# Pairwise comparisons in a router's top-k selection, and a scatter split around the last up products

## Chip, core and metric

One NeuronCore of a Trainium2 chip runs one program: an inference step of a two-layer decoder in fp32. The metric is the device time of one execution in microseconds.

## What is computed

336 tokens (16 meta and 256 prompt tokens, and 8 sequences of 8 sampled tokens) pass an RWKV-7 layer and a differential attention layer. Each of the two is followed by a mixture of experts (MoE) with the same router:

```python
s = sigmoid(xt @ router_w)                     # (336, 16)
sel = s + router_b
grp = top_k(sel.reshape(-1, 4, 4), 2)[0].sum(-1)   # best two of each group of 4
gmask = one_hot(top_k(grp, 1)[1], 4)           # the best group
eidx = top_k(where(emask, sel, -inf), 2)[1]    # its best two experts
wts = s at eidx, divided by their sum
y = sum over e of gates[:, e] * ((silu(xt @ w_gate[e]) * (xt @ w_up[e])) @ w_down[e])
```

With equal values, the lower index wins. The model width is 1024, an expert's 512. An expert's three matrices have 2 MB each, a layer's 16 experts 100 MB.

## The kernel before, in words

Each engine has its own program, written out by hand, and semaphores join them. The tokens lie in three tiles of 128, 128 and 80 rows (`TOK`). The stages are the RWKV layer, an output projection, MoE 0, keys, values and queries, attention, an output projection, MoE 1 and the output. All parts of the change lie in the two MoE stages, `experts` of each engine.

**In front of the experts.** VectorE (DVE) adds the residual to each tile (`residual`, L2179), from which ACT forms the variance (`spread_of`, L1664) and DVE the normalized rows (`normalize`, L2198). TensorE (PE) turns the tiles (`turn`, L1247) and forms the logits and their fold (`logits`, `route`). ACT takes the sigmoid. DVE's selection (L2334 to L2371) works on 128 x 48 scores, 16 experts for each of three tiles: the sum of the best two of each group as the maximum of six pair sums, then the best group and the best two experts by three calls of `first_best` (L2344), which each take a maximum, mark who equals it, weight the marks by a falling index, take the maximum and compare again. A drain stands behind nearly every small instruction. PE forms the ranks of the tokens within their expert (`ustrict`, `ones`), DVE reads them at L2391, and `select` (L2237) makes from them the 0/1 matrix `SelF`, which for four experts of 64 slots each says which token goes into which slot. Between them, DVE computes two of the remainders (`remainder`, L2287): the normalized rows are held as two fp32r parts, `XTM[0]` (hi, copied by ACT) and `XTM[1]` (lo, what is left); POOL computes the lo part of tile 0. The semaphore `xtm_lo` counts tile 2's, then tile 1's.

**Gather.** `gather(q, i)` (L1109) multiplies the parts by `SelF` into PSUM bank `i % 2`: 12 products of 256 columns, in the order hi 0, 1, 2, lo 0, 2, 1, for two of the eight chunks of the width. Four calls make one quad's input. ACT empties the banks of i = 0 and 2, DVE those of i = 1 and 3 (`gathered`, L1689 and L2242), and call i waits until the bank of i - 2 is empty.

**Experts.** Eight pairs, j = 0 to 7, each of two experts. `pair` of PE (L1173): gate products, up products, then either a scatter or the next gather, then transposes of the product of both (`HH`), of the chosen part of `SelF`, and down products. Every matrix has a slot of 16 KB a partition, seven slots in all, loaded in two halves by SP's queue; a slot is loaded again when PE is through with it (`free`, L543). SP issues in a fixed order: gate, up, down of pair after pair. For the last pair, the down matrices are loaded by halves of their columns.

**Scatter.** The outputs of pairs go back to the rows by products with `SG`, in turns (`TURNS`): pairs (0, 1), (2, 3), (4, 5), (6), (7). One turn has six parts, a tile's half each; PE writes part i into bank 6 + i % 2 once DVE's addition of part i - 2 is done (`scatter`, L1157; `adds`, L2249). Turn 3, that of pair 6, is done in pair 7: PE behind the up products, DVE behind the multiplication of gate and up (L2267). Turn 4 follows the last down products.

## Time and profile before

| | |
|---|---|
| median of 3 runs | 1219.72 us (1216.82 to 1220.41) |
| the profiled execution | 1218.88 us |
| its span | 1217.2 us |
| TensorE busy | 1081.1 us, 89% |
| VectorE busy | 541.1 us, 44% |
| ScalarE busy | 358.0 us, 29% |
| GpSimd busy | 70.0 us, 6% |
| read from HBM | 266.18 MB, 224 GB/s over the span |
| mean granted TensorE clock | 0.937 of full |
| chain that ended last | PE 74%, DVE 12%, DMA 6%, ACT 3% |

Busy shares are means over stages with different limits. The two MoE stages lie at about 412 to 682 us and 937 to 1214 us; the page's slices are 30.4 us each. PEclk and the clock column of the windows are the granted clock as a share of 2.4 GHz: 0.5 is 1.2 GHz. An fp32 product shows as two records of PE. Where a helper issues an instruction, the line is the helper's: L742 is PE's `mm`, L1484 and L1487 are ACT's, L526 is SP's weight load.

### The profile page before, as it was taken

The numbers are of one execution on the slowest core, as the hardware profiler recorded it, in microseconds if no ns is written. First come the engines' busy times: TensorE is split into PE (matmuls) and PEld (weight loads), VectorE is DVE, ScalarE is ACT, GpSimd is POOL, SyncE is SP. The second block draws the span as 40 slices with busy tenths as digits, with TensorE's granted clock in tenths as the row PEclk, the third lists the DMA queues.
The fourth block names the chain that finished last, engine by engine and source line by source line (L and its number), as shares of the span: only waits on it lengthen the run. The fifth ranks groups of instructions, "written<-read, shape, count | busy, mean of one in ns | idle before, by whom it ended". The sixth has DMA issues, their size and how long they took to land.

```text
span 1217.2 us, 23537 instructions
## 1 busy us (share of the span) xinstructions
PE 1081.1 (89%) x10193; PEld 760.0 (62%) x10194; DVE 541.1 (44%) x1068; ACT 358.0 (29%) x720; POOL 70.0 (6%) x101
## 2 busy tenths in 40 slices
PE   4989989899888869999998799999879599999984
PEld 3877978899855644555443699976636444444532
DVE  5856536556566571212122754474444631222215
ACT  3435424443232421111111533473232411111102
POOL 2002100011000000000000112011100000000000
PEclk8989979999997979999999899999989699999997
DMA  9503010011041929999999803464733289999991
GB/s 333 215 10 69 19 47 3 3 38 38 25 154 70 396 95 421 422 422 423 422 423 398 316 1 125 159 234 144 290 139 140 106 348 422 423 423 423 422 401 48
DMA packets 58251, 274.16 MB, mean 225 GB/s; under 512 B 5169, under 2 KB 5690, under 8 KB 34082
## 3 DMA queue, kind: packets, MB, share of 16 engines
q1 hardware_dynamic: 48160, 237.58, 48.6%
q0 software_dynamic: 9360, 34.72, 8.8%
q8 instruction: 83, 1.36, 0.5%
q10 hardware_dynamic: 626, 0.32, 0.1%
q14 instruction: 22, 0.18, 0.0%
HBM read 266.18 MB, written 6.46 MB: 224 GB/s over the span
## 4 chain that ended last, share of the span: by engine, by line
PE 74%; DVE 12%; DMA 6%; ACT 3%; issue 2%; DVEq 1%; SPq 0%; POOLq 0%; ACTq 0%; POOL 0%
PE ps L742 69%; DMA arena<-in_moe_w_up 5%; ACT arena L1484 2%; PE ps L883 1%; PE ps L1373 1%; DVE arena L1924 1%; DMA arena<-in_cache_k 1%; ACT arena L1487 1%; PE ps L1089 1%; PE ps L1205 1%; DVE pwr_lo L1930 0%; PE ps L1253 0%; DVE arena L2024 0%; DMA arena<-in_x_prompt 0%; DVE arena L2483 0%
## 5 line engine op out<-in xcount | busy, mean ns | idle before, releaser
L742 PE MATMUL ps<-arena 64*64 64x64 f32 (+10 forms) x7348 | 625.8, 323 | 61.8 <-DVE arena L2376 15.6
L742 PEld LDWEIGHTS ps<-arena 64*64 64x64 f32 (+4 forms) x7348 | 355.5, 140 | 309.1 <-issue 220.7
L1487 ACT COPY arena<-ps 128x512 f32<-128x512 f32 (+7 forms) x294 | 121.4, 432 | 338.8 <-PE ps L742 182.2
L2267 DVE TENSOR_TENSOR arena<-arena,ps 128x512 f32<-128x512 f32 x16 | 17.4, 1085 | 185.5 <-PE ps L742 185.5
L1484 ACT ACTIVATE arena<-ps,arena 128x256 f32<-128x256 f32 (+5 forms) x96 | 45.5, 507 | 133.5 <-PE ps L742 102.4
L2278 DVE SCALAR_TENSOR_TENSOR yy_lo<-ps,arena,yy_hi 128x512 fp32r<-128x512 f32 x32 | 22.7, 747 | 123.0 <-ACT yy_hi L1484 123.0
L1484 ACT ACTIVATE pw_hi<-arena 128x1024 fp32r<-128x1024 f32 x40 | 42.0, 1057 | 89.0 <-PE ps L742 82.8
L742 PE MATMUL ps<-px_hi,pw_hi 128*128 128x336 f32 x192 | 63.4, 330 | 1.4 <-DVE px_lo L2157 1.0
L742 PE MATMUL ps<-px_lo,pw_hi 128*128 128x336 f32 x192 | 61.9, 322 | 0.0
L742 PE MATMUL ps<-px_hi,pw_lo 128*128 128x336 f32 x192 | 61.8, 322 | 0.0
L1484 ACT ACTIVATE yy_hi<-ps,arena 128x512 fp32r<-128x512 f32 x32 | 20.5, 684 | 106.3 <-PE ps L742 106.3
L1484 ACT ACTIVATE arena<-arena 128x1024 f32<-128x1024 f32 (+9 forms) x73 | 42.9, 629 | 26.9 <-DVE arena L2176 20.6
L2146 DVE TENSOR_TENSOR pw_lo<-arena,pw_hi 128x1024 fp32r<-128x1024 f32 x24 | 29.4, 1225 | 43.2 <-ACT pw_hi L1484 43.1
L742 PE MATMUL ps<-rx_hi_hi,pwr_hi 128*128 128x336 f32 x96 | 34.3, 357 | 12.6 <-ACT rx_hi_hi L1484 8.0
L742 PE MATMUL ps<-yy_hi,sg 128*128 128x512 f32 (+1 forms) x96 | 40.4, 421 | 4.8 <-DVE arena L2256 2.7
L1930 DVE TENSOR_TENSOR pwr_lo<-arena,pwr_hi 128x1024 fp32r<-128x1024 f32 x24 | 29.4, 1223 | 33.8 <-ACT pwr_hi L1484 33.6
L742 PE MATMUL ps<-pw_hi,px_hi 128*128 128x512 f32 (+1 forms) x96 | 40.7, 424 | 4.1 <-ACT pw_hi L1484 3.8
L1484 ACT ACTIVATE arena<-ps 128x512 f32<-128x512 f32 (+4 forms) x23 | 11.4, 506 | 103.9 <-PE ps L742 103.8
L742 PE MATMUL ps<-pw_hi,px_lo 128*128 128x512 f32 (+1 forms) x96 | 39.6, 413 | 0.0
L742 PE MATMUL ps<-pw_lo,px_hi 128*128 128x512 f32 (+1 forms) x96 | 39.3, 409 | 0.0
L742 PEld LDWEIGHTS ps<-px_hi,pw_hi 128*128 128x128 f32 x192 | 37.1, 193 | 1.9 <-issue 1.9
L742 PE MATMUL ps<-yy_lo,sg 128*128 128x512 f32 (+1 forms) x96 | 37.8, 394 | 0.0
(229 smaller groups left out, 1387.3 us busy)
## 6 DMA issues: line engine op xcount, KB each, us to landing
arena<-in_moe_w_gate SPq DMA_DIRECT2D x64, 1024.0 KB, 15.7
arena<-in_moe_w_up SPq DMA_DIRECT2D x64, 1024.0 KB, 18.8
arena<-in_moe_w_down SPq DMA_DIRECT2D x64, 1024.0 KB, 17.0
arena<-in_rwkv_w_rkv SPq DMA_DIRECT2D x6, 2048.0 KB, 19.5
arena<-in_w_kv_shared SPq DMA_DIRECT2D x4, 2048.0 KB, 19.8
arena<-in_cache_k POOLq DMA_DIRECT2D x16, 512.0 KB, 4.6
arena<-in_cache_v POOLq DMA_DIRECT2D x16, 512.0 KB, 6.8
arena<-in_rwkv_w_out SPq DMA_DIRECT2D x2, 2048.0 KB, 10.3
```

The lines of the kernel that those rows point to most:

```text
L742: return pe.matmul(out, lhsT, rhs, start=start, stop=stop)
L883: m = pe.transpose(ps[:, b + hf, P * c:P * c + P], src[:, 4 * hf + c, o0:o0 + P], ident)
L1089: m = pe.transpose(ps[0:n, 4 + g % 4, P * c:P * c + P], X[:, 4 * hf + c, t0:t0 + n], ident)
L1205: m = pe.transpose(ps[:, 2, P * f:P * f + P], HH[:, P * f:P * f + P], ident)
L1373: m = pe.transpose(ps[:, 2 * g + hf, P * c:P * c + P], PGK[b % 4][:, g, P * (4 * hf + c):P * (4 * hf + c) + P], ident)
L1484: return act.activation(out, in_, func, **k)
L1487: return act.copy(out, in_)
L1924: stt(X[:, c, :], sgT[:, c, :], mixv[m][:, c:c + 1], xT[:, c, :], ALU.mult, ALU.add).then_inc(S("mix_ready"), 1)
L1930: tt(lo, w_in(L_RKV + n // 4)[:, :, P * (n % 4):P * (n % 4) + P], hi.bitcast(F32), ALU.subtract).then_inc(S("rw_lo"), 1)
L2146: tt(lo, w_in(L_KV + co // 4)[:, :, P * (co % 4):P * (co % 4) + P], hi.bitcast(F32), ALU.subtract).then_inc(S("pw_lo"), 1)
L2267: tt(HH.rearrange("p (k q) -> p q k", k=NF), HS.rearrange("p (q k) -> p q k", k=NF), bank(3).rearrange("p (q k) -> p q k", k=NF), ALU.mult ...
L2278: stt(YY[ROWS[j]][1][:, h], bank(4 + hf), gsl, YY[ROWS[j]][0][:, h].bitcast(F32), ALU.mult, ALU.subtract).then_inc(S("yl_ready"), 1)
```

## The change

Five edits, in both layers:

1. The selection compares every value with the other three of its set: `r4` holds "other > own", `g4` "other >= own", and where the other comes first `g4` replaces `r4` by a predicated copy; the sum over the others is the rank. This is done once for groups (rank below 0.5 is the best group), and once for the experts of the best group, which a product with the mask and a sum over groups picks out (rank below 1.5; -1 for rows beyond the tile). The three calls of `first_best` and the masking with large numbers go.
2. The remainders of tiles 2 and 1 on DVE move behind `select`, ahead of the counts.
3. The first two calls of the first gather are interleaved: four parts of both banks, then lo 2 of both behind the first `xtm_lo`, then lo 1 of both behind the second.
4. Residual 2 moves ahead of the normalization of tile 0 on DVE, and the variance of tile 2 ahead of the first copy of turned rows on ACT.
5. In pair 7, parts 0 to 2 of turn 3 of the scatter go ahead of the up products on PE, and ahead of the multiplication on DVE; parts 3 to 5 stay.

```diff
@@ constants and sizes @@
+PARTS = [(0, 0), (0, 1), (0, 2), (1, 0), (1, 2), (1, 1)]
-    parts["w16"], parts["w4"], parts["valid"]
+    parts["first"] = np.tile((np.arange(4)[None, :] < np.arange(4)[:, None]).reshape(1, 16), (P, 1))
+    parts["below"] = np.concatenate([np.where(p < n, 1.5, -1.0) for _, n in TOK], 1)
@@ PE gather @@
-            def gather(q, i):
-                for h, t in ((0, 0), (0, 1), (0, 2), (1, 0), (1, 2), (1, 1)):
+            def gather(q, i, order):
+                for h, t in order:
                     t0, k = TOK[t]
-                    if q % 4 == 0 and i == 0 and h and t:
-                        pe.wait_ge(S("xtm_lo"), 2 * (q // 4) + (1 if t == 2 else 2))
...
-                m.then_inc(S("xg_mm"), 1)
+                if order[-1] == (1, 1):
+                    m.then_inc(S("xg_mm"), 1)
@@ PE scatter, pair @@
-            def scatter(l, s):
+            def scatter(l, s, first=0, end=6):
...
-                for i, (t, hf) in enumerate(parts(s)):
+                for i, (t, hf) in list(enumerate(parts(s)))[first:end]:
...
                     if k == 1:
                         wait(pe, S("sg_ready"), g)
+                        if j == PAIRS - 1:
+                            scatter(l, 3, 0, 3)
...
                 if j == PAIRS - 1:
-                    scatter(l, 3)
+                    scatter(l, 3, 3, 6)
@@ PE experts @@
-                for i in range(4):
-                    if i >= 2:
-                        pe.wait_ge(S(("xga_ready", "xgb_ready")[i % 2]), 8 * l + i // 2)
-                    gather(4 * l, i)
+                for i in range(2):
+                    gather(4 * l, i, PARTS[0:4])
+                pe.wait_ge(S("xtm_lo"), 2 * l + 1)
+                for i in range(2):
+                    gather(4 * l, i, PARTS[4:5])
+                pe.wait_ge(S("xtm_lo"), 2 * l + 2)
+                for i in range(2):
+                    gather(4 * l, i, PARTS[5:6])
+                for i in range(2, 4):
+                    pe.wait_ge(S(("xga_ready", "xgb_ready")[i % 2]), 8 * l + i // 2)
+                    gather(4 * l, i, PARTS)
@@ ACT experts @@
                 spread_of(2 * l, 1)
+                spread_of(2 * l, 2)
                 turned_copy(l, 0)
-                spread_of(2 * l, 2)
@@ DVE adds, pair: first and end as in scatter @@
+                if j == PAIRS - 1:
+                    adds(l, 3, 0, 3)
                 dve.wait_ge(S("hs_ready"), g + 1)
...
                 if j == PAIRS - 1:
-                    adds(l, 3)
+                    adds(l, 3, 3, 6)
@@ DVE experts @@
                 residual(l, 1)
+                residual(l, 2)
                 normalize(2 * l, 0)
-                residual(l, 2)
...
+                def ahead(val):
+                    other = v3(val).unsqueeze(2).to_broadcast([P, 3, 4, 4])
+                    own = v3(val).unsqueeze(3).to_broadcast([P, 3, 4, 4])
+                    tt(g44(r4), other, own, ALU.is_gt)
+                    tt(g44(g4), other, own, ALU.is_ge)
+                    dve.drain()
+                    dve.copy_predicated(v3(r4), mc("first").bitcast(U32).unsqueeze(1).to_broadcast([P, 3, 16]), v3(g4))
+                    dve.drain()
+                    dve.tensor_reduce(ga, g12(r4), AX, ALU.add)
+                    dve.drain()
...
-                first_best(gb, gm, ga, G_, mc("w4"))
-                gmask = gb.unsqueeze(2).to_broadcast([P, 12, 4])
-                tsc(gc, gb, BIG, -BIG, ALU.mult, ALU.add)
-                tt(g12(a1), g12(sel), gmask, ALU.mult)
-                dve.drain()
-                tt(g12(a1), g12(a1), gc.unsqueeze(2).to_broadcast([P, 12, 4]), ALU.add)
-                dve.drain()
-                first_best(msk0, a1, a2, E_, mc("w16"))
-                stt(a1, msk0, -2 * BIG, a1, ALU.mult, ALU.add)
-                dve.drain()
-                first_best(oh, a1, a2, E_, mc("w16"))
-                tt(msk, msk0, oh, ALU.add)
-                dve.drain()
-                tt(v3(msk), v3(msk), mc("valid").unsqueeze(2).to_broadcast([P, 3, E_]), ALU.mult)
+                ahead(gm)
+                tsc(gb, ga, 0.5, None, ALU.is_lt)
+                dve.drain()
+                tt(g12(a1), g12(sel), gb.unsqueeze(2).to_broadcast([P, 12, 4]), ALU.mult)
+                dve.drain()
+                dve.tensor_reduce(v3(gm), a1.rearrange("p (t g n) -> p t n g", t=3, g=4), AX, ALU.add)
+                dve.drain()
+                ahead(gm)
+                tt(v3(gc), v3(ga), mc("below").unsqueeze(2).to_broadcast([P, 3, 4]), ALU.is_lt)
+                dve.drain()
+                tt(g44(msk), v3(gb).unsqueeze(3).to_broadcast([P, 3, 4, 4]), v3(gc).unsqueeze(2).to_broadcast([P, 3, 4, 4]), ALU.mult)
...
                 tsc(a2, msk, -1e6, 1e6, ALU.mult, ALU.add)
-                remainder(2)
                 dve.wait_ge(S("rt_pe"), 5 * l + 5)
...
                 select(4 * l)
+                remainder(2)
+                remainder(1)
                 dve.tensor_reduce(cntp[:, 0:1], ps[:, 7, 64:80], AX, ALU.max)
...
                 dve.drain().then_inc(S("route_ready"), 1)
-                remainder(1)
```

## Rows read from the trace of the kernel before

**Rows 1.** The page: the span, and what the transfers moved in 40 slices.

```profile
span 1217.2 us, 23537 instructions
...
GB/s 333 215 10 69 19 47 3 3 38 38 25 154 70 396 95 421 422 422 423 422 423 398 316 1 125 159 234 144 290 139 140 106 348 422 423 423 423 422 401 48
```

**Rows 2.** Windows, MoE 0: busy time of the engines, PEclk, DMA share, GB/s.

```profile
430.40:431.20 0.80, 0.00 (x0) 0.00 (x0) 0.58 (x4) 0.00 (x0) 0.00 (x0) 0.50 0.05 20
...
458.00:646.00 188.00, 188.00 (x1007) 93.41 (x1003) 37.42 (x53) 26.16 (x53) 0.54 (x1) 1.00 1.01 423
```

**Rows 3.** The chain that ended last, MoE 0's last pair: start, length, what.

```profile
620.89 29.45 DMA arena<-in_moe_w_up
...
650.38 8.79 PE ps L742 x30
...
659.26 1.08 DVE arena L2267
660.34 0.53 DVE arena L2254
...
661.01 0.72 PE ps L742 x2
...
662.59 1.25 PE ps L742 x4
```

**Rows 4.** Timeline of VectorE in MoE 0: selection, weights, remainder, ranks (start, length).

```profile
427.02 0.17 DVE L2346 TENSOR_REDUCE arena<-arena 128x3 f32<-128x12 f32 x1
...
429.22 0.20 DVE L2346 TENSOR_REDUCE arena<-arena 128x3 f32<-128x48 f32 x1
429.50 0.21 DVE L2348 TENSOR_TENSOR arena<-arena 128x48 f32<-128x48 f32 x1
...
432.88 0.17 DVE L2373 COPY arena<-arena 128x16 f32<-128x16 f32 x1
...
434.35 0.21 DVE L2385 TENSOR_TENSOR arena<-arena 128x48 f32<-128x48 f32 x1
434.48 0.18 DVE L2387 TENSOR_SCALAR arena<-arena 128x48 f32<-128x48 f32 x1
434.57 1.89 DVE L2292 TENSOR_TENSOR xtm_lo<-arena,xtm_hi 80x1024 fp32r<-80x1024 f32 x1
436.56 0.20 DVE L2391 TENSOR_TENSOR arena<-arena,ps 128x48 f32<-128x48 f32 x1
```

**Rows 5.** Timeline of MoE 0: ranks, gather, first evacuation, first gate products.

```profile
433.44 1.46 PE L742 MATMUL ps<-arena 128*128 128x48 f32 x6 [7.79 <-DVE arena L2376]
...
437.94 1.62 PE L742 MATMUL ps<-sel,xtm_hi 128*128 128x256 f32 x6 [3.04 <-DVE sel L2239]
...
441.15 1.02 ACT L1484 ACTIVATE arena<-ps,arena 128x256 f32<-128x256 f32 x2 [11.63 <-PE ps L742]
...
443.12 0.88 PE L742 MATMUL ps<-sel,xtm_hi 128*128 128x256 f32 x6
...
447.30 3.22 PE L742 MATMUL ps<-arena 128*64 128x512 f32 x14 [1.14 <-issue]
```

**Rows 6.** Timeline of MoE 0: normalization and turning of tiles 0 and 1.

```profile
415.71 0.81 DVE L2202 TENSOR_SCALAR arena<-arena 128x1024 f32<-128x1024 f32 x1
...
416.44 0.68 DVE L2187 SCALAR_TENSOR_TENSOR arena<-arena,ps 80x512 f32<-80x512 f32 x1
...
416.58 1.10 PE L1253 MATMUL ps<-arena 128*128 128x128 f32 x8 [1.82 <-DVE arena L2202]
...
419.03 1.97 PE L1253 MATMUL ps<-arena 128*128 128x128 f32 x8 [1.36 <-DVE arena L2202]
```

**Rows 7.** Windows, MoE 0: the gather's start; around the last up weights' landing.

```profile
437.90:442.60 4.70, 4.66 (x20) 4.50 (x21) 2.16 (x3) 1.02 (x2) 0.00 (x0) 0.50 0.00 0
...
646.00:650.00 4.00, 0.53 (x3) 0.00 (x0) 0.00 (x0) 0.60 (x1) 0.00 (x0) 1.00 1.00 415
650.00:654.00 4.00, 3.62 (x10) 1.14 (x12) 0.00 (x0) 0.00 (x0) 0.00 (x0) 0.61 1.03 387
```

More of the change, by code:

```diff
@@ L116, in constants @@
     parts["iota"] = np.tile(np.arange(CAP), (P, 1))
-    parts["w16"] = np.tile(np.arange(E_, 0, -1), (P, 1))
-    parts["w4"] = np.tile(np.arange(G_, 0, -1), (P, 1))
-    parts["valid"] = np.concatenate([p < n for _, n in TOK], 1)
+    parts["first"] = np.tile((np.arange(4)[None, :] < np.arange(4)[:, None]).reshape(1, 16), (P, 1))
+    parts["below"] = np.concatenate([np.where(p < n, 1.5, -1.0) for _, n in TOK], 1)
     parts["caus"] = np.where(q > p, -BIG, 0.0)
@@ L1194, in more_rows @@
                             pe.wait_ge(S(("xga_ready", "xgb_ready")[i % 2]), 2 * (q + 1) + i // 2)
-                            gather(q + 1, i)
+                            gather(q + 1, i, PARTS)
                 if j == PAIRS - 1:
-                    scatter(l, 3)
+                    scatter(l, 3, 3, 6)
                 elif j % 2 or j == 0:
@@ L2247, in gathered, with adds @@
                 m.then_inc(S("xgb_ready"), 1)
-            def adds(l, s):
-                for i, (t, hf) in enumerate(parts(s)):
+            def adds(l, s, first=0, end=6):
+                for i, (t, hf) in list(enumerate(parts(s)))[first:end]:
                     n, h = TOK[t][1], slice(512 * hf, 512 * hf + 512)
@@ L2329, in g12, with g44 @@
                     return x.rearrange("p (g n) -> p g n", n=4)
-                score, sel, a1, a2, oh, msk0, msk, _ = rt
+                def g44(x):
+                    return x.rearrange("p (t i j) -> p t i j", t=3, i=4)
+                score, sel, a1, a2, r4, g4, msk, _ = rt
                 gm, ga, gb, gc = gs
-                m12 = ga[:, 0:12]
+                top1 = cntf[:, 0:3]
+                def ahead(val):
[8 more added lines that the diff above has]
+                    dve.drain()
                 tt(v3(sel), v3(score), rbB.unsqueeze(1).to_broadcast([P, 3, E_]), ALU.add)
@@ L2341, in experts @@
                 dve.drain()
-                top1 = cntf[:, 0:3]
-                def first_best(dst, val, tmp, width, weight):
-                    dve.tensor_reduce(top1, v3(val), AX, ALU.max)
-                    dve.drain()
-                    tt(v3(tmp), v3(val), top1.unsqueeze(2).to_broadcast([P, 3, width]), ALU.is_equal)
-                    dve.drain()
-                    tt(v3(tmp), v3(tmp), weight.unsqueeze(1).to_broadcast([P, 3, width]), ALU.mult)
-                    dve.drain()
-                    dve.tensor_reduce(top1, v3(tmp), AX, ALU.max)
-                    dve.drain()
-                    tt(v3(dst), top1.unsqueeze(2).to_broadcast([P, 3, width]),
-                       weight.unsqueeze(1).to_broadcast([P, 3, width]), ALU.is_equal)
-                    dve.drain()
-                first_best(gb, gm, ga, G_, mc("w4"))
-                gmask = gb.unsqueeze(2).to_broadcast([P, 12, 4])
-                tsc(gc, gb, BIG, -BIG, ALU.mult, ALU.add)
-                tt(g12(a1), g12(sel), gmask, ALU.mult)
+                ahead(gm)
+                tsc(gb, ga, 0.5, None, ALU.is_lt)
                 dve.drain()
-                tt(g12(a1), g12(a1), gc.unsqueeze(2).to_broadcast([P, 12, 4]), ALU.add)
+                tt(g12(a1), g12(sel), gb.unsqueeze(2).to_broadcast([P, 12, 4]), ALU.mult)
                 dve.drain()
-                first_best(msk0, a1, a2, E_, mc("w16"))
-                stt(a1, msk0, -2 * BIG, a1, ALU.mult, ALU.add)
+                dve.tensor_reduce(v3(gm), a1.rearrange("p (t g n) -> p t n g", t=3, g=4), AX, ALU.add)
                 dve.drain()
-                first_best(oh, a1, a2, E_, mc("w16"))
-                tt(msk, msk0, oh, ALU.add)
+                ahead(gm)
+                tt(v3(gc), v3(ga), mc("below").unsqueeze(2).to_broadcast([P, 3, 4]), ALU.is_lt)
                 dve.drain()
-                tt(v3(msk), v3(msk), mc("valid").unsqueeze(2).to_broadcast([P, 3, E_]), ALU.mult)
+                tt(g44(msk), v3(gb).unsqueeze(3).to_broadcast([P, 3, 4, 4]), v3(gc).unsqueeze(2).to_broadcast([P, 3, 4, 4]), ALU.mult)
                 dve.drain()
```

## Prediction

> **What bounds the kernel now.** I read the page first, then the windows of the transfers, the chain that ended last, and the timeline around the router and around the last pair of experts. The span is 1217.2 us; the profiled execution took 1218.88 us, so 1.7 us lie around the span, and the median of the three runs, 1219.72 us, is 0.8 us above it. The change touches only the two mixture-of-experts layers. Both look alike to a few hundredths of a microsecond, the second 525 us after the first; each pattern stands once in the rows and counts twice.
>
> In the slices of the page, the transfers stand at some 420 GB/s for nearly the whole of either stage of experts [rows 1]. Ahead of that is a hole: the seven weight slots are full and next to nothing is moved (20 GB/s near 431 us), then the queue runs at 423 GB/s from 458 to 646 us [rows 2]. It can only restart when the first pair's gate products give slots back, so two things set the stage's length: when those products begin (447.30 us [rows 5]), and a fixed number of bytes after that. TensorE is busy all the while, but it ends up waiting: the chain goes through the transfer of the last pair's up weights, issued at 620.89 and landed at 650.33 us [rows 3]. TensorE did 0.53 us of work in the 4 us before that [rows 7]. So a microsecond saved **in front of pair 0** comes off the end whole, a microsecond saved between pair 0 and the landing is lost, and a microsecond saved **behind the landing** counts again. The change works in the first and the third stretch.
>
> **The selection.** Its first three steps stay. From the first maximum at 427.02 to the copy at 432.88 us are 5.86 us now, 21 small VectorE instructions [rows 4]. A step that is drained costs 0.28 us to the next one (429.22 to 429.50), one that is not drained 0.13 (434.35 to 434.48) [rows 4]. The new chain has two rounds of comparisons, each an undrained comparison, a drained one, a predicated copy and a reduction: 0.13 + 3 x 0.28 = 0.97 us; and five single drained steps: 1.40 us. Together 3.34 us, **2.5 us less**. No predicated copy is in this trace. The least it can cost is a plain copy's 0.2 us, the most I allow is 0.5 us each, so the saving lies between 2.0 and 2.7; I take the ordinary 0.28, since it handles the same 48 elements as its neighbours.
>
> **The remainder behind the selection.** The 80-row remainder now starts at 434.57 and the ranks are read only at 436.56 us, though TensorE's rank products (433.44 us plus 1.46) were done at 434.90 [rows 4, 5]. Taken out, VectorE's own steps end at about 434.6, TensorE's products decide, and the ranks are read at about 435.05: **1.5 us less**. The remainders' cost (1.89 us for this one, some 2 us for the 128-row one) goes behind the selection matrix. Queued behind them on VectorE are the counts, `route_ready` (which ACT and SP want only before pair 7, some 190 us later) and the evacuation of gathered banks 1 and 3; TensorE waits for both remainders in the gather.
>
> **The gather.** I count from its first product (now 437.94 us [rows 5]). The new order runs 16 products (four parts, two banks), then 4, then 4. At the lower clock a product costs 4.66/20 = 0.233 us, at the full one about half [rows 7]. The 16 last 3.7 us; the first remainder is ready 1.8 us in and the second 3.8 us in, wanted at 4.7. Neither is waited for. What is late next is the bank: both banks complete together, at products 22 and 24, some 5.2 us in, and bank 0 cannot be overwritten before ACT has emptied it (1.02 us [rows 5]) with 0.15 us of handshake on either side. Today ACT's work on bank 0, 441.15 to 442.17, lies beside TensorE's on bank 1, and bank 2's products begin at 443.12 us without a wait [rows 5]. Now TensorE stands some 1.1 us less the two products in between, and the clock's rise comes earlier or later within it: **1.2 us more**. Below: 0.3, if the clock rises early in the gather and the pause overlaps work that would have been slow; above: 2.2, if it rises a pause later. With VectorE's bank 1 hidden by bank 2's six products and more, nothing else is added.
>
> **The residual ahead of the normalization.** VectorE now normalizes tile 0 from 415.71 us and does residual 2 (two parts of about 0.65 us from 416.44) after it [rows 6]. Exchanged, tile 0 is normalized about 1.35 us later, tile 1 about when it is now, since both orders have the same VectorE work before it. TensorE's eight transposes of tile 0 go from 416.58 to about 418.0 and end just as those of tile 1 are due at 419.03 [rows 6]. The spare between them, 419.03 - 417.68 = 1.35 us, is what hides the move; it is used up entirely. The first eight took 1.10 us and the second eight, behind a pause, 1.97 [rows 6]: nearly twice, as at half the clock. If the clock has already fallen when tile 0 is turned, its transposes take 1.97 us and push everything behind by 0.9. ACT's square of tile 2 comes 1.1 us earlier, but TensorE is busy without a gap from 419.03 until the logits, so nothing is won with it. Between -0.1 and +1.0 a layer; I take **0.3 more**.
>
> Up to the first gate product that is -2.5 - 1.5 + 1.2 + 0.3 = **-2.5 us a layer**.
>
> **The split scatter.** Three of six parts go where TensorE waits for the last up weights, 646 to 650.4 us [rows 3, 7]. At 0.46 us of products each, and one wait for an addition, they need about 2.2 us of a hole of some 4: free, as long as the weights bound the stage. Behind the up products, all six now take from 659.1 (the first products start beside VectorE's multiplication at 659.26) to 663.84 us, because each part waits for additions that queue behind that multiplication (1.08 us, then 0.53 before the third part may start at 661.01; the last four products end at 663.84) [rows 3]. With three parts left, parts 3 and 4 find their banks free. Part 5 waits for one addition behind the multiplication and starts where the third part does now, at 661.0; its two products take about 0.5, and the transposes that follow start at 661.5 to 661.6 in place of 663.84: **2.2 us less**. Below: 1.5, if the weights of the down products are late next, as they land behind the up weights at the same rate; above: 2.5.
>
> **The clock behind the landing.** TensorE's granted clock was 1.00 in the idle stretch and 0.61 over 650 to 654 us, and the 30 records of up products took 8.79 us [rows 3, 7]. A mean of 0.61 means 3.1 of the 4 us at 1.2 GHz (0.39/0.50 x 4), and I add 0.3 us for what reaches beyond 654; at 2.4 GHz half of these 3.4 us would be saved: 1.7 us. With three parts and one up product in the hole, TensorE idles some 1.5 us at its end and 0.5 within, in place of 3.9. Where the pause was of 1.1 us, between the gather and the first gate product, the clock stayed up (14 records in 3.22 us from 447.30 [rows 5]); here half of the stretch is idle, between the two cases. I take it as kept in one layer of two: **-1.7 us in all**, bounds 0 and -3.4.
>
> A rule of the Trainium skill speaks against this term. TensorE: Matmul & The Clock Gate, section A second HAM failure mode: psum-queue depth-cycling, says that small idle stretches between groups of matmuls can bring the clock down again though none of them is long. By it the term would be 0, and the gather's new pause would cost more. The measured window above, idle at 1.00 and 0.61 behind it, cannot decide between them.
>
> **Sum.** 2 x (-2.5 - 2.2) - 1.7 = -11.1 us. From 1218.9 of the profiled execution to 1207.8, and with the 0.8 us of the median, **1208.6 us**.
>
> **Rivals.**
> - *The clock is kept in both layers* and rises early in the gather: -9.4 - 3.4, and up to 1.5 from the gather, -14.3: 1205.4. For it: the hole is half filled with work. Against: 0.61 today. Chance 0.2.
> - *The clock is the worse for the new pauses*: no gain behind the landing, and the transposes of tile 0 slow in both layers (0.7 more each): -9.4 + 1.4 = -8.0, 1211.7. This is where the skill's rule leads. Chance 0.16.
> - *The front is hidden*: the queue's restart hangs on something other than pair 0's products, so that only -4.4 of the scatter and -1.7 of the clock come through, -6.1: 1213.6. Against it is the empty queue at 431 us with the slots full [rows 2]. Chance 0.06.
> - *The split does not fit*: the three parts aren't done before the up weights land, or the down weights are late behind them; the scatter's gain is halved, -8.9: 1210.8. Against: 0.53 us of work in the 4 us [rows 7]. Chance 0.05.
> - *Slower*: the pause behind the gather's 24th product keeps TensorE at 1.2 GHz through the rest of the gather and pair 0's gate products. The gather's 48 products would then take 11.2 us for about 8.2 now, and the gate products, some 6.9 us at full clock, twice that, and each microsecond of these delays the freeing of slots and so the transfers. Net in front: -4.0 + 3.0 + 1.2 + 0.3 + 6.9 = +7.4, less 2.2 behind: +5.2 a layer, 1230. It decides from the point where the lower clock lasts 2 x 4.7 = 9.4 us longer a layer than now. Against: the clock is at 0.50 for the 4.7 us [rows 7] and then rises while products run. Chance 0.03.
>
> **How the numbers follow.** The forecast holds 0.5. A measurement of this kernel tells some 0.3%, 3.7 us, from no change. Forecast, both clock rivals and the misfit all lie beyond it, as does nearly all of the hidden front: faster 0.94, the same 0.04, slower 0.02 (the slower rival, less the part of it that ends within 0.3%). The unknown costs add up to about 3 us either way around 1208.6, and the clock rivals reach 1205.4 and 1211.7; with a margin on the side of small gains for a term left out, the range is 1203.5 to 1213.5.
>
> **What would show it.** In the changed profile: from the third step's end to the copy of the mask some 3.3 us in place of 5.9; the ranks read within 0.2 us of TensorE's products; 24 gather products without a wait and then one of about 1 us on ACT; the first gate product 2 to 3 us nearer to the end of the output projection; the landing of the last up weights earlier by the same; six scatter products ahead of it, and the transposes 2.4 us behind the last up product. The forecast is wrong if the queue does not restart earlier, if the comparisons take over 0.4 us a step, or if the granted clock in the gather or in pair 0 is 0.5 for much longer than now.

## The result and the profile after

| | before | after |
|---|---|---|
| median, runs of the same chip | 1218.27 us (1215.59 to 1220.41, 4 runs) | 1203.84 us (1199.09 to 1204.48, 4 runs) |
| the profiled execution | 1218.88 us | 1203.65 us |
| its span | 1217.2 us | 1201.9 us |
| mean granted TensorE clock | 0.937 | 0.949 |

The ratio is 0.9875, with a 95% interval of 0.985 to 0.9901. The kernel is faster by 14.4 us in the medians and by 15.3 in the spans, where 11.1 were forecast; 1203.84 lies 0.3 us above the low end of the range.

The page of the changed kernel, its span and its transfers in 40 slices, answers to [rows 1]:

```profile
span 1201.9 us, 23503 instructions
...
GB/s 332 209 23 70 1 66 3 3 38 38 26 120 65 361 144 408 423 423 423 423 423 404 385 12 92 165 216 148 270 209 68 184 338 422 422 423 423 422 412 84
```

The transfers run at the same rate; in both stages the queue comes back sooner behind its hole. To see what was saved where, I cut each MoE stage at nine points that both traces have: the start of its first residual, the first step of the selection, the sum behind the mask's copy (it releases the rank products), the reading of the ranks, the first product of the gather, the first gate product, the landing of the last up weights, VectorE's multiplication behind the up products, and the transposes behind that. Durations in us, first and second layer:

| stretch | before | after | difference, both |
|---|---|---|---|
| residual to selection | 13.85, 13.94 | 13.67, 12.56 | -1.56 |
| selection, up to the sum behind the mask's copy | 7.22, 7.20 | 5.02, 4.67 | -4.73 |
| that sum to ranks read | 3.35, 3.34 | 1.80, 1.85 | -3.04 |
| ranks to the gather's first product | 1.38, 1.38 | 1.38, 1.39 | 0.0 |
| gather, to the first gate product | 9.36, 9.44 | 10.42, 9.89 | +1.5 |
| gate product to landing | 203.04, 202.80 | 203.07, 202.82 | +0.05 |
| landing to multiplication | 8.92, 8.94 | 7.23, 7.23 | -3.4 |
| multiplication to transposes | 4.42, 4.41 | 2.25, 2.24 | -4.35 |

The sum is -15.5 us, and +0.2 lie outside these stretches. The row of 203 us is worth reading first: what is saved in front passes the stretch bound by transfers whole, as the forecast had it. The first gate product comes 2.9 and 4.9 us nearer to the first residual, where 2.5 were forecast for each layer: the two layers, alike before, no longer are.

The selection, on VectorE's timeline in the first MoE stage, with the second round of comparisons (compare [rows 4]; start, length):

```profile
428.97 0.21 DVE L2370 TENSOR_TENSOR arena<-arena 128x48 f32<-128x48 f32 x1 [0.43 <-issue]
429.25 0.23 DVE L2372 TENSOR_REDUCE arena<-arena 128x12 f32<-128x48 f32 x1
429.56 0.21 DVE L2352 TENSOR_TENSOR arena<-arena 128x48 f32<-128x48 f32 x1
429.68 0.20 DVE L2353 TENSOR_TENSOR arena<-arena 128x48 f32<-128x48 f32 x1
429.96 0.22 DVE L2355 COPY_PREDICATED arena<-arena 128x48 f32<-128x48 uint32 x1
430.25 0.20 DVE L2357 TENSOR_REDUCE arena<-arena 128x12 f32<-128x48 f32 x1
430.52 0.17 DVE L2375 TENSOR_TENSOR arena<-arena 128x12 f32<-128x12 f32 x1
...
431.05 0.17 DVE L2379 COPY arena<-arena 128x16 f32<-128x16 f32 x1
```

The predicated copy takes 0.22 us, and 0.29 to the next step: a drained step like its neighbours. The round goes as costed: 0.12, 0.28, 0.29 and 0.27 from start to start. A pause of 0.43 us waits for nothing that the profile names. From the first comparison to the mask's copy are 3.65 us here and 3.30 in the second layer, which has no such pause; 3.34 were forecast. Before, the selection had one in either layer (0.41 and 0.37).

The gather, in the same stage (compare [rows 5]; the bracket is the idle time ahead of the row and what ended it):

```profile
434.56 1.62 PE L742 MATMUL ps<-sel,xtm_hi 128*128 128x256 f32 x6 [1.49 <-DVE sel L2247]
435.98 0.63 PE L742 MATMUL ps<-sel,xtm_lo 128*128 128x256 f32 x2
436.40 1.48 PE L742 MATMUL ps<-sel,xtm_hi 128*128 128x256 f32 x6
437.68 2.33 PE L742 MATMUL ps<-sel,xtm_lo 128*128 128x256 f32 x10
...
439.63 1.02 ACT L1492 ACTIVATE arena<-ps,arena 128x256 f32<-128x256 f32 x2 [9.74 <-PE ps L742]
...
440.70 0.98 PE L742 MATMUL ps<-sel,xtm_hi 128*128 128x256 f32 x6 [0.69 <-ACT arena L1492]
```

Twenty-four products run without a wait (6 + 2 + 6 + 10), so neither remainder is late. Then TensorE stands 0.69 us for ACT, in the second layer 0.88. The clock is at 0.50 up to the pause (six products take 1.48 us) and at 1.00 behind it (0.98 for the first six, 0.88 for the next).

The transposes of the tiles, first and second layer (compare [rows 6]):

```profile
418.29 2.83 PE L1254 MATMUL ps<-arena 128*128 128x128 f32 x16 [2.99 <-DVE arena L2210]
```

```profile
936.71 2.05 PE L1254 MATMUL ps<-arena 128*128 128x128 f32 x16 [2.91 <-DVE arena L2210]
```

Sixteen transposes in one burst take the place of eight, a pause, and eight at the lower clock. In the second layer the burst runs at the full clock throughout; in the first the clock falls within it (0.70 over 418.3 to 421.1 us), and the burst takes 0.78 us more. That is what the forecast had not seen coming.

The hole ahead of the last up weights and what follows: TensorE's timeline, then the windows (compare [rows 7]; columns as there), then the chain that ended last (compare [rows 3]):

```profile
644.20 0.50 PE L742 MATMUL ps<-yy_hi,sg 128*128 128x512 f32 x1
...
645.80 0.47 PE L742 MATMUL ps<-yy_hi,sg 128*128 128x512 f32 x1 [0.41 <-DVE arena L2262]
646.11 0.40 PE L742 MATMUL ps<-yy_lo,sg 128*128 128x512 f32 x1
646.43 1.07 PE L742 MATMUL ps<-arena 128*64 128x512 f32 x2
```

```profile
644.00:648.00 4.00, 3.10 (x9) 1.16 (x8) 1.97 (x3) 0.60 (x1) 0.00 (x0) 1.00 1.01 414
648.00:652.00 4.00, 3.90 (x18) 1.35 (x20) 0.00 (x0) 0.00 (x0) 0.00 (x0) 1.00 1.04 386
```

```profile
618.21 29.84 DMA arena<-in_moe_w_up
...
648.10 7.09 PE ps L742 x30
...
655.28 1.07 DVE arena L2277
656.36 0.53 DVE arena L2262
...
657.02 0.67 PE ps L742 x2
657.69 0.44 PE ps L1206 x4
```

Three parts of the scatter lie in the hole, TensorE works 3.10 of the 4 us and the granted clock stays 1.00 behind the landing: the same 30 records take 7.09 us in place of 8.79. Behind the multiplication one part waits for an addition, and the transposes follow 2.4 us after the last up product. (The chain's piece of the transposes starts 0.16 us behind the first of them on the timeline, from which the table counts, before as after.)

### The profile page after: what moved, and what is told of

Same layout as the page of the kernel before. It is cut to its first block, busy times and chain, and to the rows that moved or that the text cites. A ratio compares the mean times of both kernels' runs of the same rounds, so it can differ in the third digit from the quotient of the medians.

```text
span 1201.9 us, 23503 instructions
## 1 busy us (share of the span) xinstructions
PE 1075.0 (89%) x10193; PEld 755.6 (63%) x10194; DVE 537.5 (45%) x1052; ACT 358.0 (30%) x720; POOL 70.2 (6%) x101
## 3 DMA queue, kind: packets, MB, share of 16 engines
q8 instruction: 83, 1.36, 0.5%
## 4 chain that ended last, share of the span: by engine, by line
PE 75%; DVE 11%; DMA 6%; ACT 3%; issue 2%; DVEq 1%; SPq 0%; POOLq 0%; ACTq 0%; POOL 0%
PE ps L742 69%; DMA arena<-in_moe_w_up 5%; ACT arena L1492 2%; PE ps L883 1%; PE ps L1381 1%; DVE arena L1932 1%; DMA arena<-in_cache_k 1%; ACT arena L1495 1%; DVE arena L2195 1%; PE ps L1089 1%; PE ps L1206 1%; DVE pwr_lo L1938 0%; DMA arena<-in_x_prompt 0%; DVE arena L2032 0%; PE ps L1254 0%
## 5 line engine op out<-in xcount | busy, mean ns | idle before, releaser
L2262 DVE TENSOR_TENSOR arena<-arena,ps 128x512 f32<-128x512 f32 (+1 forms) x48 | 32.5, 684 | 23.7 <-PE ps L742 23.7
```

The lines of the kernel that those rows point to most:

```text
L2262: tt(YT[0:n, t, h], YT[0:n, t, h], ps[0:n, 6 + i % 2, :], ALU.add).then_inc(S("add_done"), 1)
```

## The experiments

What the sum left open, in questions. Is the clock behind the landing kept because the hole is filled, and is the split's own gain apart from that? Did the residual's move save time, and why? What does the gather pay to the wait for its bank, to the remainders and to the clock? Each kernel has one trace and several times; the durations below are those of its trace, first and second layer. The runs stand on three chips, and each ratio is to the kernel before on the same chip. Whole runs of one kernel spread over 4.5 to 11 us, in parts that no edit touches: over the fourteen traces the first residual of MoE 0 starts at 407.2 to 413.5 us, and 269 to 277 us lie between the last pair's transposes of MoE 0 and the first residual of MoE 1. So the stretches decide, and the medians support them only roughly. The changed kernel was run once more, as it is, on the chip of the three experiments that take one edit back each (the split, the residual's move, the remainders).

> The changed kernel again, beside the others on the same chip. Both theories: 14 us below the kernel before, ratio 0.988. It also gives another look at the stretch in front of the selection: theory A (the forecast's: the residual put ahead costs TensorE time, 0.3 us a layer) expects 13.9 us or more from the first residual (end of the output projection) to the first step of the selection in either layer; theory B (the two turns of tiles now follow each other without a pause and gain by it, more where the clock has not fallen before they begin) expects 12.5 to 13.7 us.

It took 1202.32 us (1200.93 to 1206.08, 4 runs), ratio 0.9869 (0.9846 to 0.9891): the same within the spread. Residual to selection was 13.64 and 12.55, the gather 10.26 and 9.98, landing to multiplication 7.23 in both.

### The hole ahead of the up weights

**Without the split.** All six parts behind the up products again, on TensorE and VectorE:

```diff
-                        if j == PAIRS - 1:
-                            scatter(l, 3, 0, 3)
...
-                    scatter(l, 3, 3, 6)
+                    scatter(l, 3)
...
-                if j == PAIRS - 1:
-                    adds(l, 3, 0, 3)
...
-                    adds(l, 3, 3, 6)
+                    adds(l, 3)
```

> The changed kernel with all six parts of the scatter behind the up products again. If the empty hole makes the clock fall (theory B), the up products take 8.8 us again in place of 7.1, and the transposes begin 4.7 us behind them in place of 2.5: 3.9 us a layer, 7.8 in all slower than the changed kernel. If the 1.7 us came by chance (theory A: one layer of two), the up products take 7.1 us in at least one layer, and it is 4.4 to 6.1 us slower.

It took 1209.40 us (1206.65 to 1211.19, 6 runs), ratio 0.9928 (0.9909 to 0.9947). TensorE's timeline and the windows on both sides of the landing:

```profile
647.26 10.10 PE L742 MATMUL ps<-arena 128*64 128x512 f32 x30 [3.77 <-DMA arena<-in_moe_w_up]
```

```profile
643.00:647.00 4.00, 0.49 (x4) 0.00 (x0) 0.00 (x0) 0.60 (x1) 0.00 (x0) 0.94 1.00 414
647.00:651.00 4.00, 3.74 (x10) 1.24 (x12) 0.00 (x0) 0.00 (x0) 0.00 (x0) 0.50 1.04 388
```

With the hole empty, landing to multiplication takes 10.25 and 10.12 us, more than the 8.92 and 8.94 of before: the clock fell earlier here, already ahead of the landing. Multiplication to transposes is 4.42 again in both layers. By these stretches the kernel loses 10.3 us, by the medians on this chip 7.1.

**The hole filled, the scatter whole.** To part the two effects, six products that nobody reads went into the hole, into banks 0 and 1, which are idle in the last pair (the parts would write 6 and 7), and the scatter stayed whole behind the up products (edits of the previous kernel, and):

```diff
-                            scatter(l, 3, 0, 3)
+                            for i in range(6):
+                                mm(ps[:, i // 3, :], XTM[0][0][:, 0:128], XTM[0][0][:, 0:512])
```

> The changed kernel with the scatter whole behind the up products, and six products that nobody reads (fp32r, 512 columns) in the hole ahead of the landing instead. It parts the two gains of the split. If the filled hole keeps the clock up, the up products take 7.2 us to the start of VectorE's multiplication (10.1 to 10.3 with the hole empty), and the transposes begin 4.4 us behind it: 4.4 us in all slower than the changed kernel, some 3.5 to 6 faster than the one with the whole scatter and the empty hole. If the early additions themselves made the up products faster, they take 8.9 or more.

It took 1207.88 us (1200.46 to 1211.31, 6 runs), ratio 0.9897 (0.9865 to 0.9929).

```profile
643.22 1.65 PE L742 MATMUL ps<-xtm_hi 128*128 128x512 f32 x6
644.80 1.07 PE L742 MATMUL ps<-arena 128*64 128x512 f32 x2
647.11 7.08 PE L742 MATMUL ps<-arena 128*64 128x512 f32 x30 [1.23 <-DMA arena<-in_moe_w_up]
```

Landing to multiplication is 7.23 in both layers, multiplication to transposes 4.42. So the two gains are separate: **work in the hole keeps the clock, though nobody reads it** (1.7 us a layer against the kernel before, 2.9 to 3.0 against the empty hole of the previous run), even with 1.23 us idle at its end; and **moving three parts** gives 2.17 us. By the medians the pair is less clean: the stretches make it 5.9 us, the ratios 3.8, with intervals that overlap. So this rests on the stretches, which agree in both layers.

### The residual ahead of the normalization

**The old order,** on VectorE and ACT:

```diff
-                spread_of(2 * l, 2)
                 turned_copy(l, 0)
+                spread_of(2 * l, 2)
...
-                residual(l, 2)
                 normalize(2 * l, 0)
+                residual(l, 2)
```

> The changed kernel with residual 2 and the variance of tile 2 back in their old places. Theory A: 0.6 us faster than the changed kernel. Theory B: slower than it by 0.4 to 2.8 us (0.2 to 1.4 a layer), with 13.8 to 13.9 us from the first residual to the selection in both layers, two groups of eight transposes with a pause of 1.3 us between them.

It took 1206.68 us (1203.36 to 1210.41, 6 runs), ratio 0.9905 (0.9885 to 0.9924), 4.4 us above the changed kernel beside it. Its timeline and the windows of the stretch:

```profile
417.88 1.10 PE L1254 MATMUL ps<-arena 128*128 128x128 f32 x8 [1.82 <-DVE arena L2210]
420.34 1.97 PE L1254 MATMUL ps<-arena 128*128 128x128 f32 x8 [1.36 <-DVE arena L2210]
...
424.51 3.60 PE L742 MATMUL ps<-arena 128*32 128x128 f32 x40
```

```profile
417.00:420.30 3.30, 1.10 (x8) 0.86 (x8) 3.13 (x9) 2.69 (x5) 0.00 (x0) 0.85 1.00 415
420.30:429.00 8.70, 8.29 (x76) 6.64 (x76) 3.56 (x8) 4.65 (x7) 2.87 (x1) 0.50 1.02 422
```

Residual to selection is 16.07 and 13.89. The second layer is back at the 13.94 of before; the first is 2.2 us worse than before, with the same instructions in front: the clock falls in the same place (1.97 for the second eight transposes) but stays at 0.50 through the 40 products of the logits, which take 3.60 us. In the trace of before these took 2.09:

```profile
422.74 2.09 PE L742 MATMUL ps<-arena 128*32 128x128 f32 x40
```

The second gather suffers too, 11.82 against 9.98. So in these traces the edit gains 1.3 to 1.4 us in the second layer and between 0.2 and 2.4 in the first. How long the clock stays down once it has fallen is not settled by the work in front alone. The two halves of the edit, VectorE's and ACT's, were not taken apart.

**The pause filled.** Four products that nobody reads (an identity by 384 columns of constants, into a bank not yet in use) ahead of the transposes:

```diff
+            def keep(b, n):
+                for _ in range(n):
+                    mm(ps[:, b, 0:384], ident, common[:, 0:384])
...
+                keep(7, 4)
                 turn(0)
```

> The changed kernel with four fp32 products of 384 columns that nobody reads between the output projection and the first turn of a tile. Theory B (the residual's place gains because the turns start at the higher clock or raise it): sixteen transposes in 2.05 us in both layers (2.8 to 3.5 in the first layer now), and 12.6 us from the first residual to the selection in both, 1.1 less in the first layer. If the clock is not what sets the first layer's 13.6, the transposes get faster and the 13.6 stay.

It took 1201.61 us (1199.15 to 1204.76, 5 runs), ratio 0.9853 (0.9825 to 0.9881).

```profile
413.69 2.75 PE L742 MATMUL ps<-arena 128*128 128x384 f32 x8
416.84 2.06 PE L1258 MATMUL ps<-arena 128*128 128x128 f32 x16 [0.40 <-DVE arena L2215]
```

Residual to selection becomes 12.58 and 12.57. The 1.1 us by which the first layer of the changed kernel lags behind its second is the clock, all of it.

The other traces can be counted in the same way. In the old order (the kernel before, and two kernels here) the clock fell within the transposes in all six layers. With the move and nothing in the pause it fell in all seven first layers, where the sixteen take 2.80 to 3.46 us, and in one of seven second layers, that of the kernel with the plain gather further down:

```profile
933.14 2.57 PE L1254 MATMUL ps<-arena 128*128 128x128 f32 x16 [2.91 <-DVE arena L2208]
```

There residual to selection was 13.62, only 0.3 us better than the old order; in the other six it was 12.55 to 12.57. With the pause filled the clock fell in none of eight layers. The move alone thus makes the fall rarer, and filling the pause prevented it each time.

### The gather

**Remainders and order as before.**

```diff
-                for i in range(2):
-                    gather(4 * l, i, PARTS[0:4])
+                gather(4 * l, 0, PARTS[0:4])
...
-                for i in range(2):
-                    gather(4 * l, i, PARTS[4:5])
+                gather(4 * l, 0, PARTS[4:5])
...
-                for i in range(2):
-                    gather(4 * l, i, PARTS[5:6])
+                gather(4 * l, 0, PARTS[5:6])
+                gather(4 * l, 1, PARTS)
...
+                remainder(2)
                 dve.wait_ge(S("rt_pe"), 5 * l + 5)
...
-                remainder(2)
-                remainder(1)
...
                 dve.drain().then_inc(S("route_ready"), 1)
+                remainder(1)
```

> The changed kernel with the remainders where they were and the gather in its old order; only selection, residual and scatter remain changed. Both theories: ranks read 3.3 us behind the mask in place of 1.8, so 1.5 us a layer lost, and the gather's pause of 1.1 us gone; 1 to 2 us slower than the changed kernel in all. A rival by which the pause is worth more than the remainders would have it faster.

It took 1204.99 us (1199.41 to 1206.50, 6 runs), ratio 0.990 (0.9881 to 0.992). Copy to ranks is 3.35 and 3.67, the gather 8.95 and 9.71. Residual to first gate product is 32.38 and 32.02, against 32.29 and 30.36 of the changed kernel: moving the remainders saves 1.5 to 1.8 us ahead of the ranks, but the gather takes 1.5 of it back in the first layer and 0.2 in the second. Net: 0.1 and 1.7. The medians on this chip are 2.7 us apart, with intervals that overlap.

**The old order with the late remainders** (the first of the two hunks alone):

> The changed kernel with the remainders behind the selection matrix, but the first gather in its old order, bank 0 whole before bank 1. If the interleaving is what makes room for the late remainders, bank 0's ten products end 2.3 us in and wait until 3.9 for the second remainder, and the first gate product comes 10.8 to 11.4 us behind the gather's start in place of 9.9 to 10.4: 1.5 to 2.5 us slower than the changed kernel. The rival, that the interleaving only moves a pause (on ACT in place of on the remainder), expects no difference.

It took 1204.37 us (1202.76 to 1208.01, 5 runs), ratio 0.9892 (0.9867 to 0.9917).

```profile
435.80 1.16 PE L742 MATMUL ps<-sel,xtm_lo 128*128 128x256 f32 x4
437.99 0.80 PE L742 MATMUL ps<-sel,xtm_lo 128*128 128x256 f32 x2 [1.03 <-DVE xtm_lo L2300]
```

The gather takes 11.77 and 12.08, more than I had expected: TensorE waits 1.03 us for the second remainder, and the clock rises only late in the third bank. By the stretches interleaving is worth 1.4 and 2.2 us, the second with part of the clock in it: it stayed at 0.50 for 9.4 us of this gather, and for 3.7 of the changed kernel's. The medians don't tell the two kernels apart (ratios 0.9892 and 0.9875, intervals overlapping).

**Four banks in place of two.** The third and fourth calls write banks 4 and 5, free at that time, and wait for nobody; ACT and VectorE empty those:

```diff
-            def gather(q, i, order):
+            def gather(q, i, order, b=0):
...
-                        m = mm(ps[:, i % 2, o:o + QUAD], XTM[h][t][0:k, P * c:P * c + P],
+                        m = mm(ps[:, i % 2 + b, o:o + QUAD], XTM[h][t][0:k, P * c:P * c + P],
...
                 for i in range(2, 4):
-                    pe.wait_ge(S(("xga_ready", "xgb_ready")[i % 2]), 8 * l + i // 2)
-                    gather(4 * l, i, PARTS)
+                    gather(4 * l, i, PARTS, 4)
```

> The changed kernel with banks 2 and 3 of the first gather put into PSUM banks 4 and 5, so that no product waits for ACT. If the wait is the bank alone, the gather takes 9.2 to 9.4 us to the first gate product in place of 9.9 to 10.4, and nothing else moves: 1 to 2 us faster than the changed kernel. If instead ACT's and VectorE's own evacuations set the end (the rival), it stays at 9.9 or more.

It took 1200.41 us (1194.17 to 1202.75, 6 runs), ratio 0.9836 (0.9808 to 0.9864).

```profile
438.13 2.30 PE L742 MATMUL ps<-sel,xtm_lo 128*128 128x256 f32 x10
440.27 0.88 PE L742 MATMUL ps<-sel,xtm_hi 128*128 128x256 f32 x6
```

The pause is gone and the gather takes 9.43 and 9.00: 1.0 and 0.9 us less. The rival, evacuations that set the end, expected no gain. In the first layer that is nearly all of the 1.06 that the gather had lost; in the second it is twice the 0.45, so there the wait was not all that had changed.

**Four banks, the old order of the normalization** (both edits as above), to see the residual's move without the pause behind it:

> The kernel with banks 4 and 5, and with the residual and the variance back in their old places: two more looks at the stretch from the first residual to the selection without that edit, at other moments of the clock. Theory B (it keeps the clock from falling or staying down): 13.8 us where the clock rises in the logits, 15 to 16 where it does not, never the 12.6 of the edit; some 2 to 5 us slower than with banks alone. Theory A: no slower than with banks alone.

It took 1204.03 us (1199.32 to 1206.20, 6 runs), ratio 0.9874 (0.9848 to 0.99). Residual to selection is 16.07 and 13.92, against 13.68 and 12.56 with the move. The 16.07 of the first layer is therefore no accident of one trace, and the 40 products of the logits take 3.60 us again.

### The clock in front of the experts

**Four banks and the filled pause ahead of the transposes:**

> The changed kernel with banks 4 and 5 in the first gather and the four idle-time products ahead of the turns: 12.6 us from the first residual to the selection and 9.0 to 9.4 from the gather to the gate products in both layers. 1.9 us shorter in the shares plus 1.1 of the first layer: 3 us faster than the changed kernel, 17 to 18 below the kernel before.

It took 1199.84 us (1194.99 to 1203.19, 6 runs), ratio 0.9841 (0.9813 to 0.9868), not measurably apart from four banks alone. Residual to selection is 12.59 and 12.58, the gather 9.86 and 8.99. What is gained ahead of the selection is partly paid back in the first gather (9.43 before): the clock falls during the selection in any case.

**Filled behind the logits as well,** in the changed kernel with its two banks:

```diff
                 route(2).then_inc(S("rt_pe"), 1)
+                keep(3, 7)
                 pe.wait_ge(S("rt_dve"), 6 * l + 6)
...
                 mm(ps[:, 7, 64:64 + E_], ones, running[:, 48:64]).then_inc(S("rt_pe"), 1)
+                keep(3, 1)
```

> The same, with seven more such products behind the logits and one behind the ranks, so that TensorE works through the selection. If the clock's fall in the selection is what makes the ranks and the gather slow: ranks' products in 0.8 us in place of 1.46, 24 gather products then in 3.7 to 4.1 us (bounded by the second remainder, 3.8 us behind the selection matrix) in place of 4.5 to 5.1; 2 us a layer from the mask to the first gate product, 4 us in all, faster than the changed kernel together with the turns' 1 us. If the filler is in the way of the ranks, they are read later than 1.8 us behind the mask.

It took 1201.07 us (1195.48 to 1203.09, 6 runs), ratio 0.9847 (0.9819 to 0.9875). The gather's first row, then the window around its start:

```profile
431.19 1.62 PE L742 MATMUL ps<-sel,xtm_hi 128*128 128x256 f32 x6 [1.09 <-DVE sel L2254]
```

```profile
429.90:432.50 2.60, 1.51 (x7) 1.34 (x7) 2.52 (x3) 0.00 (x0) 0.00 (x0) 0.69 0.00 0
```

The clock was 1.00 from 424 to 430 us and fell all the same, in the last wait of 1.09 us for the selection matrix. The gather took 9.65 and 9.75, not the gain that I had expected. In the second layer landing to multiplication was 9.20 (7.23 in the first): TensorE's first product of the last pair came 3.31 us late, a delay that the trace puts down to its own sequencer, so the parts of the scatter began only as the weights landed and the up products stood behind them.

**Everything:** the same with two products behind the ranks in place of one, four banks, and the first five parts of the third bank's call ahead of the last remainder:

```diff
+                keep(3, 2)
...
                     gather(4 * l, i, PARTS[4:5])
+                gather(4 * l, 2, PARTS[0:5], 4)
                 pe.wait_ge(S("xtm_lo"), 2 * l + 2)
                 for i in range(2):
                     gather(4 * l, i, PARTS[5:6])
...
+                gather(4 * l, 2, PARTS[5:6], 4)
+                gather(4 * l, 3, PARTS, 4)
```

> The same and seven idle-time products through the selection, two behind the ranks, and the gather's four banks ordered by what the remainders allow. If the clock stays up into the gather: 7.0 to 7.6 us from its first product to the gate products in place of 9.0 to 9.4, 4 us in all faster than with banks and warm turns. If the clock falls ahead of the gather all the same (as with one product behind the ranks), 9 us or more and no gain.

It took **1194.20 us** (1192.41 to 1198.77, 5 runs), ratio 0.9812 (0.9785 to 0.9838), which lies wholly below the interval of the changed kernel.

```profile
428.83 0.95 PE L742 MATMUL ps<-sel,xtm_hi 128*128 128x256 f32 x6 [0.45 <-DVE sel L2254]
...
436.13 13.95 PE L742 MATMUL ps<-arena 128*64 128x512 f32 x64 [1.14 <-issue]
```

```profile
427.00:436.00 9.00, 7.55 (x52) 6.37 (x52) 7.56 (x14) 2.86 (x5) 0.00 (x0) 1.00 0.01 3
```

The wait ahead of the gather is 0.45 us (0.78 in the second layer), the clock 1.00 throughout, and the gather takes 7.30 us in both layers. Residual to first gate product is 27.8 in both, against 32.3 and 30.4. What the fillers and the new order of the gather each give was not measured apart.

## Where the prediction held, and the step that failed

**What bounds the kernel: right.** In both layers of all fourteen traces gate product to landing is 202.6 to 203.3 us, whatever was saved in front. The rival of the hidden front is refuted.

**The selection: right,** -4.7 against -5.0 for both layers. The predicated copy cost an ordinary step; the pause of 0.43 us makes up the rest. No run takes the selection back alone, so this is read from its stretch.

**The remainder: right ahead of the ranks,** -3.04 against -3.0.

**The gather: right in kind, too large.** The 24 products without a wait and then ACT's bank came as written, but the term was +1.2 a layer and the table shows +1.06 and +0.45. The pause is 0.69 and 0.88 us, where the signs named about 1. That the wait costs this much is shown by the four banks, which give back 1.0 and 0.9. What made the second layer's gather lose only 0.45 is read from the windows and not tested: the clock is at 0.50 for its first 5.3 and 3.7 us, against 4.7 and 5.0 before.

**The residual's move: the step that failed.** The text said that the spare of 1.35 us "is used up entirely", allowed -0.1 to +1.0 and took +0.3. Both layers together gave -1.56 where +0.6 was forecast, 2.2 us off and with the wrong sign. VectorE's timing was right: tile 0 is normalized later and the 16 transposes join. What was wrong is "nothing is won with it": the move could gain. [Rows 6] showed both halves: the first eight transposes in 1.10 us, the second eight in 1.97 behind a pause. I priced the move against that trace's slow transposes as if they were given, though the move takes away the very pause. Filling the idle time ahead of them (12.58 and 12.57) and the old order (16.07 and 13.89; 16.07 and 13.92) show the clock as the cause. How much the move gains depends on whether the clock falls all the same: 0.2 to 2.4 us in the first layer and 0.3 to 1.4 in the second. That the whole came out at 15.3 is in part luck of the trace; with the 13.62 that one second layer had, this stretch alone would have made it 14.2.

**The split: right,** -4.35 against -4.4.

**The clock behind the landing: the mechanism right, the size half.** I took it as kept in one layer of two; it was kept in both, -3.4 in place of -1.7. The hole was idle for 0.41 and 0.59 us, less than the 0.5 and 1.5 that I had, and the filled hole with the whole scatter shows that work in the hole is enough even with 1.23 us idle at its end. The Trainium skill's rule named in the prediction, that small idle stretches between groups of matmuls can bring the clock down (TensorE: Matmul & The Clock Gate, section A second HAM failure mode: psum-queue depth-cycling), was read as losing this term. With idle stretches of 0.41 and 0.59 us in the hole the trace disagrees with that reading: 1.00 in both windows. Ahead of the experts the traces agree with it in kind: in the old order of the normalization the clock went to 0.50 behind idle stretches of 1.82 and 1.36 us around a burst of 1.10 us.

Together: the clock at the landing -1.7, the residual's move -2.2, the gather -0.9, the selection +0.3, and 0.25 elsewhere. From -11.1 this is -15.3, the difference of the spans. Of the rivals, the clock kept in both layers was nearest, at 1205.4; it put its further 1.5 us in the gather, which gave only 0.9, and did not see the residual. The other rivals' marks did not appear: the gather is at 0.50 for 0.6 us longer than before in one layer and 1.2 us less in the other, the gate products run at 1.00, and no part of the scatter is late.

**Open:** why the clock, once down, came back before the logits in the trace of before and stayed down in two traces with the same instructions ahead of them; why it fell in every first layer of the changed order without a filler and in one second layer of seven, behind nearly the same idle time (2.99 and 2.91 us); and where the delay of 3.31 us at the last pair in one trace comes from. No run told these apart.

## What to carry to other kernels

Where a latency-bound chain has short bursts of TensorE between waits, price an edit by what it does to the pauses, not only by the moved work: a term may change sign if it joins two bursts. A hole that waits for a transfer is worth filling twice over, for the work and for the clock behind it; here work that nobody reads served for the second. Before adding a wait on a bank, look for banks that are idle in that stage. And fill up to the last wait: here the clock, at 1.00 for the 6 us before, fell in one of 1.09 us.

## What was not expected of the hardware

- The clock fell without any one long pause: behind 1.82 us idle, 1.10 busy, 1.36 idle it was 0.50, while behind a single pause of 2.91 us it stayed 1.00 in six second layers of seven (in the first layers, behind 2.99 us, it fell). It also stayed with 0.99 and 0.45 us idle around 2.23 us of products, and with 1.23 us idle ahead of the up products behind a filled hole.
- The lower clock lasts differently long behind the same work: the 40 logit products took 2.09 us in one trace and 3.60 in two others, of the same instructions.
- A predicated copy of 128x48 fp32 took 0.22 us, against 0.21 for a comparison of the same shape.
